# Order of the context's sums, factors and spare weight parts in the two-stream tails of a diffusion block

## The reference

```python
def rmsnorm(x, g):
    return x * rsqrt(mean(x * x, -1) + EPS) * g
def modulate(h, g_pre, shift, scale):
    return rmsnorm(h, g_pre) * (1 + scale) + shift
def gated_residual(h, y, g_post, gate, weight):
    return h + weight * gate * rmsnorm(y, g_post)
def swiglu_half(h, m, k, g_pre, g_post, wg, wu, wd):
    u = modulate(h, g_pre, m[3 * k], m[3 * k + 1])
    y = (silu(u @ wg) * (u @ wu)) @ wd
    return gated_residual(h, y, g_post, m[3 * k + 2], 0.5)
for i in range(2):
    x, ctx = swiglu_half(x, ...), swiglu_half(ctx, ...)          # ffn 0
    ctx = gated_residual(ctx, mixer(modulate(ctx) @ w_in) @ w_out)   # not in the last layer
    x = gated_residual(x, mixer(modulate(x) @ w_in) @ w_out)
    x, ctx = swiglu_half(x, ...), swiglu_half(ctx, ...)          # ffn 1, ctx not in the last layer
```

## Time and profile before

| what | value |
|---|---|
| median of 3 runs | 2171.79 us (2170.77 to 2173.74) |
| the profiled execution's own time | 2169.65 us |
| its span | 2167.9 us |
| mean granted TensorE clock | 0.98 of full speed |
| TensorE (PE) busy | 95% of the span, 11565 matmuls |
| VectorE (DVE) busy | 63% |
| ScalarE (ACT) busy | 40% |
| GpSimd (POOL) busy | 17% |
| two-stream tails, first matmul of the context pair | 423.41, 877.25, 1264.49, 1643.78 us |

### The profile page before, as it was taken

How to read it: one execution, slowest core, us unless ns; L and a number is a source line. 1 busy time by engine, 2 the same in 40 slices (tenths; PEclk the granted TensorE clock), 3 DMA queues, 4 the chain that set the end, 5 groups by cost and what they waited for, 6 DMA issues and landing times. The chain is left out here.

```text
span 2167.9 us, 28865 instructions
## 1 busy us (share of the span) xinstructions
PE 2059.9 (95%) x11565; PEld 1734.8 (80%) x11565; DVE 1367.7 (63%) x2107; ACT 859.6 (40%) x1464; POOL 359.7 (17%) x315
## 2 busy tenths in 40 slices
PE   6999999999889989999999999999999978899998
PEld 4888787987556778888878898888889757889998
DVE  4888874558777553688777752223737779555444
ACT  3322322436455343422222342222235635544443
POOL 0111100134112400111110021111003433301210
PEclk9999999999999989999999999999999999999999
DMA  7555553313223213255555513332531334344553
GB/s 285 195 179 186 192 199 112 120 51 106 70 86 117 78 58 117 78 194 193 189 183 190 177 58 109 98 97 97 186 116 42 98 103 150 99 136 136 178 183 127
DMA packets 251091, 291.06 MB, mean 134 GB/s; under 512 B 9342, under 2 KB 211022, under 8 KB 250958
## 3 DMA queue, kind: packets, MB, share of 16 engines
q1 hardware_dynamic: 249927, 286.95, 40.0%
q10 hardware_dynamic: 1031, 2.28, 0.3%
HBM read 288.02 MB, written 1.18 MB: 133 GB/s over the span
## 5 line engine op out<-in xcount | busy, mean ns | idle before, releaser
L185 PE MATMUL bank<-uh,split 128*128 128x512 f32 (+1 forms) x2016 | 731.1, 363 | 21.3 <-ACT xbc_pad L1620 6.2
L186 PE MATMUL bank<-ul,split 128*128 128x512 f32 (+1 forms) x2016 | 713.1, 354 | 0.0
L187 PE MATMUL bank<-uh,split 128*128 128x512 f32 (+1 forms) x2016 | 712.8, 354 | 0.0
L115 DVE TENSOR_TENSOR split<-raw,split 128x1024 fp32r<-128x1024 f32 (+1 forms) x296 | 355.7, 1202 | 484.4 <-ACT split L106 477.1
L106 ACT ACTIVATE split<-raw 128x1024 fp32r<-128x1024 f32 (+1 forms) x280 | 289.7, 1035 | 765.9 <-PE bank L187 755.6
L185 PEld LDWEIGHTS bank<-uh,split 128*128 128x128 f32 x2016 | 383.3, 190 | 94.7 <-issue 25.4
L187 PEld LDWEIGHTS bank<-uh,split 128*128 128x128 f32 x2016 | 383.3, 190 | 52.8
L186 PEld LDWEIGHTS bank<-ul,split 128*128 128x128 f32 x2016 | 383.7, 190 | 52.1 <-issue 3.1
L249 DVE SCALAR_TENSOR_TENSOR mod_acc<-raw_mod,cond,mod_acc 128x512 f32<-128x512 f32 x448 | 329.1, 794 | 0.0
L1100 POOL TENSOR_TENSOR hl<-hf,hh 128x512 fp32r<-128x512 f32 (+1 forms) x88 | 131.4, 1493 | 790.9 <-ACT hh L1111 790.9
L185 PE MATMUL bank<-hh,split 128*128 128x512 f32 (+1 forms) x740 | 254.2, 343 | 2.5 <-DVE split L115 2.4
(11 more groups left out here) (247 smaller groups left out, 2344.4 us busy)
## 6 DMA issues: line engine op xcount, KB each, us to landing
raw_mod<-in_w_mod SPq DMA_DIRECT2D x128, 512.0 KB, 5.4
raw<-in_ffn_w_gate SPq DMA_DIRECT2D x44, 1024.0 KB, 5.3
raw<-in_ffn_w_up SPq DMA_DIRECT2D x44, 1024.0 KB, 5.1
raw<-in_w_in SPq DMA_DIRECT2D x40, 1024.0 KB, 5.1
raw<-in_ffn_w_down SPq DMA_DIRECT2D x32, 1024.0 KB, 4.8
raw<-in_w_out SPq DMA_DIRECT2D x16, 1024.0 KB, 4.7
raw<-in_ffn_w_down SPq DMA_DIRECT2D x16, 768.0 KB, 4.2
decay<-cum_rows SPq DMA_DIRECT2D x48, 256.0 KB, 3.6
```

The lines of the kernel that those rows point to most:

```text
L115: ins = K.nc.vector.tensor_tensor(wl[:, half, 0:kn, :], K.raw[:, slot, 0:kn, half * P:half * P + P], r32(wh[:, half, 0:kn, :]), ALU.subtract)
L185: K.nc.tensor.matmul(bank[:, 0:tn], wh[:, half, k, :], h, start=first and k == 0, stop=False)
L186: K.nc.tensor.matmul(bank[:, 0:tn], wh[:, half, k, :], l, start=False, stop=False)
L187: ins = K.nc.tensor.matmul(bank[:, 0:tn], wl[:, half, k, :], h, start=False, stop=last and k == kn - 1)
```

## The change

Three hand-written orders are altered, in every two-stream tail. On TensorE the four sums of the context's new residual go behind k blocks 4, 5, 6 of the last panel's first latent half and 0 of its second (before: 5, 6, 0, 1), the context's factors behind block 3 of the second (before: 5), and the latent sums behind step 2 of the pair (before: 1). On ScalarE the high part of context tile 2 goes ahead of the latent `tile(1, 1)`. On VectorE the low part of spare half 3 goes ahead of the context's second reciprocal, `tile_squares(1, 1)` behind `low(0, 2)`, and the latent reciprocal behind `low(0, 4)`. No instruction is added or removed.

```diff
--- before.py
+++ after.py
@@ -722,17 +722,17 @@
                     self.factors_pe(pe, 0)
 
             def first_squares_after(k):
-                if k >= 5:
-                    self.square_sum_pe(pe, 0, k - 5)
+                if k >= 4:
+                    self.square_sum_pe(pe, 0, k - 4)
 
             def last_squares_after(k):
-                if k < 2:
-                    self.square_sum_pe(pe, 0, 2 + k)
-                elif k == 5:
+                if k == 0:
+                    self.square_sum_pe(pe, 0, 3)
+                elif k == 3:
                     self.factors_pe(pe, 0, 2)
 
             def latent_norm_after(step):
-                if step == 1:
+                if step == 2:
                     if self.mods:
                         pe.wait_ge(K.mod_evac.sem, K.mod_evac.at(self.mod_group + 1))
                     self.sums_pe(pe, 1)
@@ -858,9 +858,9 @@
             spare_half(3)
             tile(1, 0)
             root(0, 2)
-            shifted(0, 0, 2)
+            shifted(0, 0, 3)
             tile(1, 1)
-            shifted(0, 2, 4)
+            shifted(0, 3, 4)
             root(1, 1)
             shifted(0, 4, 8)
             squares(1, 0, 8)
@@ -953,21 +953,21 @@
             for n in range(4):
                 pair(0, n)
             head_lo(K, dve, K.nc.vector, 2, nth)
+            head_lo(K, dve, K.nc.vector, 3, nth)
             factors(0, 2)
             tile_squares(1, 0)
             normed(0, 0)
             normed(0, 1)
-            head_lo(K, dve, K.nc.vector, 3, nth)
             low(0, 0)
-            tile_squares(1, 1)
             normed(0, 2)
             low(0, 1)
             normed(0, 3)
             low(0, 2)
+            tile_squares(1, 1)
             normed(0, 4)
-            factors(1, 1)
             normed(0, 5)
             low(0, 4)
+            factors(1, 1)
             normed(0, 6)
             normed(0, 7)
             low(0, 6)
```

## The result

The changed kernel takes 2157.89 us in the median of 4 runs (2152.82 to 2159.17), the kernel before on the same chips 2171.28 (2169.96 to 2173.74): a ratio of 0.9933, 95% interval 0.9914 to 0.9951. Five later runs gave 2158.42, ratio 0.994 (0.9928 to 0.9953). The forecast was 2161, so a gain of 10.8 us where 13.4 were measured, 13.1 in the later runs; both medians lie at the low end of the range, 2157 to 2167.

The account below looks back on a forecast made before the run. TensorE, 95% busy, was bound by waits for VectorE's low parts and its lower clock in four context pairs. Gain 13.9 us less two clock falls is 10.6; 2171.79 minus that is 2161.2, predicted 2161, range 2157 to 2167.

Parts of the forecast that it names:

- steps 1 to 6: First tail, from the context's sums to the end of its pair: pair of 8.76 us, gain 13.9 if the clock holds.
- Steps 1 and 2: Context sums one block forward, and spare low part 3 ahead of VectorE's reciprocal with 0.62 us margin: both cost nothing.
- The sum: Whole kernel: 10.6 us off the profiled 2169.65 gives 2159.05; off the median 2171.79 gives 2161.2; predicted median 2161.
- 1 us of run spread: Low end of the range: taken off 2157.9, the time with no clock fall, to reach 2157.
- two of four: TensorE's clock falls in two of the four tails' context pairs, at most 1.65 us each: gain 10.6 us.
- gain of 13.9: Four context pairs at 35.0 us against 48.90, if TensorE keeps its clock in every tail.
- 0.2 to spare: Behind the context pair: VectorE's first latent pair sum done at 431.35, TensorE wants it at 431.58; priced at nothing.
- a wait ahead of L353: Sign of a wrong forecast: TensorE waiting ahead of the factors or the sums.
- (b): Rival: two-input VectorE and GpSimd passes collide on each tail's path, 2.9 us off the forecast, gain 7.7, 2164; chance 0.10.
- (a): Rival: TensorE's clock falls in every tail, gain 7.3 us, 2164.5; chance 0.17.
- (c): Rival: latent chain waits 1.4 us a tail (5.6) and the clock falls in each; 1.7 remains, 2170; chance 0.09.
- (d): Rival: spare part 3 waits for ScalarE's high part and delays the reciprocal; at 5 us late 2177; chance 0.04.

Follow-up runs that it names:

- fill_before: Kernel before plus small matmuls that nobody reads, put where TensorE would wait in the context pair: 2163.11 us, ratio 0.9961.
- later: Changed kernel with the latent stream's four square sums one k block later on TensorE, factors where they are: 2157.77 us, ratio 0.9935.
- alone_latent: Kernel before plus small matmuls in the context pair and, of the change, only the latent stream's steps: 2166.03 us, one run.
- alone_spare: Kernel before plus small matmuls in the context pair and, of the change, only spare low part 3 ahead of the reciprocal: 2160.29 us, one run.
- alone_sums: Kernel before plus small matmuls in the context pair and, of the change, only the context's sums and factors forward: 2159.98 us, one run.
- undo_latent: Changed kernel with the latent stream's steps on TensorE, ScalarE and VectorE back where they were before: 2162.25 us, ratio 0.9956.
- undo_sums: Changed kernel with the context's four sums and its factors on TensorE back where they were before: 2165.68 us, ratio 0.9969.
- undo_spare: Changed kernel with spare low part 3 back behind the context's normed tiles 0 and 1 on VectorE: 2163.58 us, ratio 0.9971.

## Why the prediction was right and where it was not

**The path** (steps 1 to 6) was right nearly to the row. With 0.33 us added for the later start, it said 421.52, 422.14, 422.93, 423.72, 425.27 and 426.06 for the first low part, blocks 0 to 3 and the latent factors, and 430.47 for the end; the trace has 421.54, 422.17, 422.87, 423.65, 425.24, 426.05 and 430.50. Steps 1 and 2 cost nothing, as priced: the reciprocal still waits 0.62 us behind the spare parts, just the margin given. One thing there was luckier than its words: the late latent half used up all of ScalarE's free time (its root at 418.86 follows the latent tile with no idle time), so more would have cost.

**A part's worth** was not forecast for each, and experiments had to give it, in us a pair: 0.58, 0.71 and next to nothing alone, 0.86, 0.7 (from the first wait) and 0.44 as the last one added. The forecast took all three as gains. The latent steps are hardly one: their 0.44 in the pair comes with 0.36 more in the stretch behind it.

**The sum.** The step that failed is its last one, from the profiled execution to the median. For the profiled execution the forecast was 2159.05 us, and 2158.57 came. It was right in its main term too, the pairs: 10.6, of which 10.76 were measured. The distance of 2.1 us by which the profiled execution of before lay under its median was then carried over unchanged, "which minus 10.6 is 2161.2". Measured, the profiled execution of the changed kernel lies 0.7 us over its median (0.2 over that of all nine runs). So the +2.1 was -0.7, and that is 2.8 of the 3.3 us between 2161.2 and 2157.89. The half us that is left hides larger parts, which cancel: the mixer's 2.3 by chance, against it the stretches' 0.9 and 1.1 at the two ends.

What moved the medians by 13 us where the rows of two executions have 11 is in part the clock, but how far stays open. A fall does not cost the same each time: 1.40, 1.46, 2.28 and 2.10 us in the pairs of before (the pairs less those of fill_before), 1.4 to 1.5 in the changed kernel, so the "1 us of run spread" was too little. The record also has the mean granted clock of each run. Over 30 runs of the kernel before it is 0.979 (0.977 to 0.981), in its profiled execution 0.980; over nine runs of the changed kernel 0.984 (0.983 to 0.986), in the profiled one 0.983. At two levels, full and half, that is some 25 us less at half rate for the runs, against 12 between the two profiled executions. So by its clock the profile of before was a light one and that of after a heavy one, in the direction of the 2 to 3 us. That it is these us is not shown: among the runs of the kernel before the time hardly follows the clock (2169.32 us at 0.981, 2173.96 at 0.980), and no row tells which falls the runs without a kept profile had. Adding up 6.5 for the path and 8.1 for the clock, less the 1.3 to 1.8 that is left, does not show it either: these are differences of the same medians and must give 13.

**The clock.** The count, two of four, was in part luck. Both profiled executions of the changed kernel have it, but the run named later, the same up to the end of the pair, has none. And the gain of 13.9, meant as that of no fall at all, bounds nothing: it counted the falls of one execution, and 13.4 came with two falls still in the profile.

**What is late next** was named in the right place and priced wrong. "0.2 to spare" before the first latent pair sum, priced at nothing, became a wait: one of the forecast's own signs of being wrong, a wait ahead of L353. The stretch grew from 8.07 to 8.52 us in both tails that kept the clock, 0.9 in all. In the forecast's terms: VectorE's first pair addition began at 431.34, 0.08 later than worked out, and took 0.91 us instead of 0.41, inside GpSimd's last residual pass, 431.24 to 431.97. It ended 0.28 behind that pass. So 0.2 to spare became 0.4 too late, and the sum stands 1.81 us behind the pair's end instead of 1.44. That is rival (b)'s collision in another place than I gave it. Before, the first addition began at 433.24 and was through in 0.42 (the first of the four in the earlier trace rows); GpSimd's last pass ended at 433.35, so the two hardly met. The Trainium skill's rule (SBUF — State Buffer, Who interferes with whom) fits: a VectorE instruction with two inputs in SBUF contends with a GpSimd instruction that reads SBUF, and the one issued first goes first. The trace agrees with it here and in the row of 0.66 us of the kernel before, whose low part began at 427.83 within a pass that ended at 428.21, and ended itself at 428.49, again 0.28 behind. That row's 0.18 is gone after the change. I had summed the collision as 0.18 for low parts and not looked at VectorE's residual work, whose pair additions moved by 2.2 us against the 1.6 of GpSimd's residual.

The collision is not the whole cause. With the clock held in the order of before (fill_before) the first addition collides too (0.73 to 0.75 us in all four tails), and the sum does not wait, as VectorE starts the addition 0.76 us behind the start of the pair's last matmul; in the changed kernel it is 0.96. So VectorE's lateness of 0.2 us, theory A of the run named later, and the longer collision are both in the wait. It came with the latent steps: alone_latent has it in all three tails that kept the clock in the pair (1.93 to 1.95 from the start of the last matmul to the sum), alone_spare, alone_sums and undo_latent in none (1.56 to 1.58). And it came only where the clock held: after a fall TensorE arrives late enough.

**The rivals.** (a) did not occur in the changed kernel's profiles, but undo_sums shows that it was not far: 0.72 us more of waiting, and all four tails fell in its one profile. (b) is real, but with VectorE's lateness it makes 0.9 us in all, not 2.9, and beside the pair, not in it. (c) is right in kind, those 0.9 us, and far too large in its 5.6; it also adds two losses that no tail of any profile had together, the fall in the pair and the wait behind it. (d) needed the spare part's high half late; it was there, as the earlier trace rows had it.

## What to carry to other kernels

Look for idle time on an engine upstream of a critical wait, and move what stands in the path into it; check by the rows that its own input is there, and that whatever waits for a second engine does not stand in front. Price the clock apart from the path, by filling TensorE's waits with matmuls that nobody needs: it tells how much of a stall is the wait and how much the lower clock behind it, and where it is worth more than it costs, keep it. Before believing "nothing in the way" where two chains close up, check for each pair of VectorE and GpSimd instructions that now overlap whether the VectorE one reads two operands from SBUF while the GpSimd one reads SBUF too. And measure a part's worth from the pair to the end of what follows it: the latent steps gained 0.44 us in the pair and lost 0.36 behind it.

## What the runs showed of the hardware

- The clock fell without any long wait. The pairs of before waited 3.0 us in parts, with at most 1.9 us at a time, and fell in four of four tails; in the changed kernel the longest idle row ahead of a block is 0.58 to 0.64 us, and two of four fell in both profiled executions. The blocks of all four pairs start at the same distances to within 0.01 us up to the fall, some 3 us behind the first block, and in the run named later none of the four fell. So the waits alone do not decide it, and for a kernel near that point a gain by the clock is a matter of odds for each pair. What decides between equal pairs no run here was made to show.
- The fall can cost more than the delay that it comes with. 0.86 us more of waiting (undo_spare) came with falls in three pairs of four, 0.72 us more (undo_sums) in four, in one profiled execution each, at 1.3 to 2.7 us a fall beside pairs of 9.65 and 9.5 us (the second one worked out).
- Work added to an engine that is busy 95% of the time made the kernel 8.1 us faster in the median (fill_before; 5.9 to 11.3 by its interval).
- A VectorE addition of 128x256 that began within a GpSimd pass ended 0.28 us behind the pass, with 0.91 us in place of 0.41, and the profile shows no idle time for it: only the row is longer.
